# A two-block transformer kernel on one core: negated maxima straight from the masking operation, embedding rows split during the MLP, and the first tables in two loads

## The reference, cut to what matters

```python
# first block, window attention: a softmax with one more "sink" score per head
s = jnp.where(mask, q @ k * d ** -0.5, -jnp.inf)
m = jnp.maximum(jnp.max(s, axis=-1, keepdims=True), sink)
pexp = jnp.exp(s - m)
probs = pexp / (jnp.sum(pexp, axis=-1, keepdims=True) + jnp.exp(sink - m))
# first block, the end of each layer: a gated embedding
gate = jax.nn.sigmoid(_rms_norm(x, ple_norm_g[l]) @ w_ple_gate[l])
e = _rms_norm(p[l] @ w_ple_proj[l], ple_post_norm_g[l])
x = x + gate * e
# second block: three kinds of causal attention, each a softmax over masked scores
p = jax.nn.softmax(jnp.where(kpos <= qpos, s, -jnp.inf), axis=-1)
```

## Time and profile before

| | us |
|---|---|
| median of 3 runs | 3013.02 |
| the profiled execution, its own time | 3004.78 |
| its span, first to last instruction | 3002.9 |
| TensorE busy | 2822.8 (94%) |
| VectorE busy | 1621.1 (54%) |
| ScalarE busy | 1113.5 (37%) |

### The profile page before, as it was taken

One profiled execution on the slowest core, in us unless ns is written; L12 is line 12 of the kernel. 1 busy time (PEld: TensorE's weight loads), 2 busy tenths in 40 slices (PEclk: granted clock), 3 DMA queues, 4 the chain that ended last, 5 costly groups with the idle time before them and its releaser, 6 DMA issues. The chain is left out here.

```text
span 3002.9 us, 37176 instructions
## 1 busy us (share of the span) xinstructions
PE 2822.8 (94%) x14756; PEld 2343.2 (78%) x14756; DVE 1621.1 (54%) x2849; ACT 1113.5 (37%) x1680; POOL 209.8 (7%) x224
## 2 busy tenths in 40 slices
PE   5998899999899889999989999899998998899998
PEld 5877788887788677888777877788887887788887
DVE  5745566655765547655575434553544544464443
ACT  6444322224554433222354444332323344332232
POOL 1320100002120210000120000100000000100001
PEclk9987999999999799999989999999999999999999
DMA  4210154443221014444422110223223210122321
GB/s 154 73 43 29 52 187 168 162 150 117 101 78 57 15 57 168 146 162 168 147 88 84 56 33 25 85 90 105 96 78 105 71 41 27 61 98 73 117 81 67
DMA packets 42835, 278.81 MB, mean 93 GB/s; under 512 B 5928, under 2 KB 6312, under 8 KB 11560
## 3 DMA queue, kind: packets, MB, share of 16 engines
q1 hardware_dynamic: 42664, 276.44, 26.4%
HBM read 274.33 MB, written 2.10 MB: 92 GB/s over the span
## 5 line engine op out<-in xcount | busy, mean ns | idle before, releaser
L307 DVE TENSOR_TENSOR low_panels<-raw_panels,high_panels 128x2048 fp32r<-128x2048 f32 (+3 forms) x218 | 469.3, 2153 | 346.0 <-ACT high_panels L294 345.8
L294 ACT ACTIVATE high_panels<-raw_panels 128x2048 fp32r<-128x2048 f32 (+3 forms) x218 | 392.5, 1802 | 469.0 <-PE bank L1516 150.0
L425 PE MATMUL bank<-mlp_h_high,high_panels 128*128 128x512 f32 x1152 | 451.4, 392 | 0.0
L425 PE MATMUL bank<-mlp_h_high,low_panels 128*128 128x512 f32 x1152 | 450.2, 391 | 0.0
L425 PE MATMUL bank<-mlp_h_low,high_panels 128*128 128x512 f32 x1152 | 448.7, 390 | 0.0
L425 PEld LDWEIGHTS bank<-mlp_h_high,low_panels 128*128 128x128 f32 x1152 | 216.3, 188 | 46.0
L425 PEld LDWEIGHTS bank<-mlp_h_low,high_panels 128*128 128x128 f32 x1152 | 216.4, 188 | 45.9
L425 PEld LDWEIGHTS bank<-mlp_h_high,high_panels 128*128 128x128 f32 x1152 | 216.4, 188 | 44.3
L450 PE MATMUL bank<-high_panels,h_high 128*128 128x256 f32 x704 | 206.5, 293 | 0.5 <-ACT values_and_ones L2033 0.5
L425 PE MATMUL bank<-h_high,high_panels 128*128 128x512 f32 x496 | 204.6, 412 | 0.5 <-DVE h_low L1401 0.3
L1516 PE MATMUL bank<-mlp_hid_high,high_panels 128*128 128x512 f32 x512 | 202.5, 395 | 0.0
(11 more groups left out here) (345 smaller groups left out, 5130.4 us busy)
## 6 DMA issues: line engine op xcount, KB each, us to landing
raw_panels<-in_w SPq DMA_DIRECT2D x236, 1024.0 KB, 4.8
raw_panels<-in_w SPq DMA_DIRECT2D x16, 384.0 KB, 3.2
raw_panels<-in_w SPq DMA_DIRECT2D x4, 960.0 KB, 4.6
raw_panels<-in_w SPq DMA_DIRECT2D x4, 768.0 KB, 4.2
row<-in_row SPq DMA_DIRECT2D x2, 1220.0 KB, 6.2
x<-in_xT SPq DMA_DIRECT2D x2, 1024.0 KB, 6.2
raw_panels<-in_w SPq DMA_DIRECT2D x4, 512.0 KB, 3.6
mix<-in_rope SPq DMA_DIRECT2D x2, 1024.0 KB, 6.2
```

The costliest lines, as they stand in the source:

```text
L294: self.nc.scalar.activation(self.g.high[:, j % SPLIT, 0:raw.shape[1]], raw, ACT.Copy).then_inc(self.high_ready, 1)
L307: self.nc.vector.tensor_tensor(self.g.low[:, j % SPLIT, 0:w], raw, self.g.high[:, j % SPLIT, 0:w].bitcast(F32), ALU.subtract).then_inc(sel ...
L425: ins = nc.tensor.matmul(bank[:, :], w[a][:, k, c0:c0 + P], rhs[b][:, k0 + k, :], start=first and k == 0 and j == 0, stop=last and k == kt ...
```

## The change

It has four parts. (1) In both attentions the mask-and-maximum instruction now multiplies by the negated scale and takes a minimum, so it gives the negated scaled maximum itself; in the window attention the minimum starts from the negated sink. The small VectorE instructions behind it are gone, ScalarE waits for each maximum by itself, and the sinks' exponentials are two ScalarE instructions of one column. (2) The embedding rows are loaded and split in `mlp_one`. (3) In the embedding stage TensorE makes two of the eight embedding groups ahead of the spread of the norm. (4) Start-up loads only the last 8 columns of `k1` and splits only the first panel; the rest of `k1` and the vectors are loaded in the first layer's stage, and the second panel is split inside its norm.

```diff
-                sp.dma_start(k1[:, :], a["k1"]).then_inc(s("tables_loaded"), 16)
+                sp.dma_start(k1[:, L_FREQ:L_WIDTH], a["k1"][:, L_FREQ:L_WIDTH]).then_inc(s("tables_loaded"), 16)
...
-                sp.wait_ge(s("vectors_loaded"), 16 * (2 * DEPTH + 1))
...
-                for i in range(AHEAD):
-                    views[0].low(dve, i)
+                views[0].low(dve, 0)
...
-                for i in range(AHEAD):
-                    views[0].high(act, i)
+                views[0].high(act, 0)
...
@@ layer_one, SP @@
+                if l == 0:
+                    sp.dma_start(k1[:, 0:L_FREQ], a["k1"][:, 0:L_FREQ]).then_inc(s("masks_loaded"), 16)
...
                 pan.loads(sp, AHEAD, 16 + AHEAD)
...
@@ layer_one, window softmax, ACT @@
-                    act.wait_ge(w.neg_ready, p + 1)
                     for m in range(2):
+                        act.wait_ge(w.max_ready, 2 * p + m + 1)
                         o = masked[:, (2 * p + m) % 6, 0:n]
-                        nc.scalar.activation(o, o, ACT.Exp, bias=g.negmax[:, 2 * p + m:2 * p + m + 1], scale=HD ** -0.5).then_inc(w.probs_ready, 1)
-                    act.wait_ge(s("sink_span"), p + 1)
-                    nc.scalar.activation(spans[:, p % 4, :], spans[:, p % 4, :], ACT.Exp).then_inc(s("sink_exp"), 1)
+                        nc.scalar.activation(o, o, ACT.Exp, bias=g.negmax[:, 2 * p + m:2 * p + m + 1], scale=-1.0).then_inc(w.probs_ready, 1)
+                    if p >= 4:
+                        act.wait_ge(w.out_kept, p - 3)
+                    for m in range(2):
+                        c = R_SINK + 2 * j + m
+                        nc.scalar.activation(spans[:, p % 4, m:m + 1], row[:, c:c + 1], ACT.Exp,
+                                             bias=g.negmax[:, 2 * p + m:2 * p + m + 1]).then_inc(s("sink_exp"), 1)
...
-                norm_scalar(nc, act, g, e, hh)
+                norm_scalar(nc, act, g, e, hh, before={3: lambda: pan.high(act, 1)} if l == 0 else None)
...
@@ layer_one, window softmax, DVE @@
-                                                       scale=1.0, scalar=NEG, op0=ALU.add, op1=ALU.max,
-                                                       accum_out=g.rowmax[:, c + m:c + m + 1]).then_inc(w.max_ready, 1)
-                    dve.wait_ge(w.max_ready, c + 2)
-                    st.link(nc.vector.tensor_tensor(g.rowmax[:, c:c + 2], g.rowmax[:, c:c + 2], sinks[:, 2 * j:2 * j + 2], ALU.max))
-                    nc.vector.tensor_scalar(g.negmax[:, c:c + 2], g.rowmax[:, c:c + 2], -HD ** -0.5, None, ALU.mult).then_inc(w.neg_ready, 1)
-                    dve.wait_ge(w.neg_ready, p + 1)
-                    nc.vector.tensor_tensor(spans[:, p % 4, :], g.negmax[:, c:c + 2], row[:, R_SINK + 2 * j:R_SINK + 2 * j + 2], ALU.add).then_inc(s("sink_span"), 1)
+                                                       scale=-HD ** -0.5, scalar=sinks[:, 2 * j + m:2 * j + m + 1], op0=ALU.add, op1=ALU.min,
+                                                       accum_out=g.negmax[:, c + m:c + m + 1]).then_inc(w.max_ready, 1)
...
-                norm_vector(nc, dve, g, e, x, vec[:, V_GIN:V_GIN + DC], hh, hl)
+                norm_vector(nc, dve, g, e, x, vec[:, V_GIN:V_GIN + DC], hh, hl, before={4: lambda: pan.low(dve, 1)} if l == 0 else None)
...
@@ mlp_one @@
+                sp.dma_start(pT[:, :, :], a["p1"][l, :, :, :]).then_inc(s("ple_in"), 16)
...
+                    if i == DC:
+                        act.wait_ge(s("ple_in"), 16)
+                        nc.scalar.activation(ph[:, :, :], pT[:, :, :], ACT.Copy).then_inc(s("p_high"), 1)
...
+                    if i == DC + 2:
+                        dve.wait_ge(s("p_high"), 1)
+                        nc.vector.tensor_tensor(pl[:, :, :], pT[:, :, :], ph[:, :, :].bitcast(F32), ALU.subtract)
...
@@ embedding_gate, PE @@
-                spread_rstd(nc, pe, g, e)
                 w = pan.parts(pe, first)
-                pe.wait_ge(s("p_low"), 1)
                 for c in range(DC):
+                    if c == 2:
+                        spread_rstd(nc, pe, g, e)
                     grp.free(pe, c)
...
@@ layer_two, softmax, ACT and DVE @@
-                    act.wait_ge(w.neg_ready, i + 1)
                     for m in range(2):
+                        act.wait_ge(w.max_ready, 2 * i + m + 1)
...
-                                                       scale=1.0, scalar=NEG, op0=ALU.add, op1=ALU.max,
...
-                    dve.wait_ge(w.max_ready, c + 2)
-                    nc.vector.tensor_scalar(g.negmax[:, c:c + 2], g.rowmax[:, c:c + 2], -u.scale, None, ALU.mult).then_inc(w.neg_ready, 1)
+                                                       scale=-u.scale, scalar=-NEG, op0=ALU.add, op1=ALU.min,
+                                                       accum_out=g.negmax[:, c + m:c + m + 1]).then_inc(w.max_ready, 1)
```

More of the change, by code:

```diff
@@ L490, in _ @@
                     sp.dma_start(lsel[:, i, :], a["lsel"][i, :, :].broadcast_to([P, 2])).then_inc(s("tables_loaded"), 16)
-                sp.dma_start(k1[:, :], a["k1"]).then_inc(s("tables_loaded"), 16)
+                sp.dma_start(k1[:, L_FREQ:L_WIDTH], a["k1"][:, L_FREQ:L_WIDTH]).then_inc(s("tables_loaded"), 16)
                 for n in range(RAW):
                     views[0].stream.load(sp, n)
-                for i in range(DEPTH):
-                    sp.dma_start(gbs[:, i, 0:3], a["gb1"][i, :, :]).then_inc(s("vectors_loaded"), 16)
-                    sp.dma_start(vec2[:, i, :], a["vec2"][i, :, :]).then_inc(s("vectors_loaded"), 16)
-                sp.dma_start(gfin[:, :], a["gfin"]).then_inc(s("vectors_loaded"), 16)
-                sp.wait_ge(s("vectors_loaded"), 16 * (2 * DEPTH + 1))
             st = Steps(s("rope_steps"))
@@ L563, in _, with layer_one @@
                     nc.scalar.activation(bounds[:, i, 3, :], bounds[:, i, 2, :], ACT.Exp)
-                for i in range(AHEAD):
-                    views[0].high(act, i)
+                views[0].high(act, 0)
         for l in range(DEPTH):
-            layer_one(nc, g, a, views[l], l, k1, vecs[:, l, :], row, gbs[:, l, :], cs, bounds[:, l, :, :], small)
-            mlp_one(nc, g, views[l], l, vecs[:, l, :])
-            embedding_gate(nc, g, a, views[l], l, vecs[:, l, :], vec2[:, l, :])
-def layer_one(nc, g, a, pan, l, k1, vec, row, gb, cs, lb, small):
+            layer_one(nc, g, a, views[l], l, k1, vecs[:, l, :], row, gbs, cs, bounds[:, l, :, :], small, vec2, gfin)
+            with ExitStack() as later:
+                pT = later.enter_context(nc.sbuf_tensor(f"ple_pT_{l}", [P, 2, S], F32))
+                ph = later.enter_context(nc.sbuf_tensor(f"ple_p_high_{l}", [P, 2, S], F32R))
+                pl = later.enter_context(nc.sbuf_tensor(f"ple_p_low_{l}", [P, 2, S], F32R))
+                mlp_one(nc, g, a, views[l], l, vecs[:, l, :], pT, ph, pl)
+                embedding_gate(nc, g, views[l], l, vecs[:, l, :], vec2[:, l, :], ph, pl)
+def layer_one(nc, g, a, pan, l, k1, vec, row, gbs, cs, lb, small, vec2, gfin):
     s, used = g.stages.begin()
+    gb = gbs[:, l, :]
     bank, x, nb = g.bank, g.x, g.nb
@@ L711, in _ @@
                 sp.dma_start(row[:, :], a["row1"][l, :, :].broadcast_to([P, R_WIDTH])).then_inc(s("in_vectors"), 16)
+                if l == 0:
+                    sp.dma_start(k1[:, 0:L_FREQ], a["k1"][:, 0:L_FREQ]).then_inc(s("masks_loaded"), 16)
+                    for i in range(DEPTH):
+                        sp.dma_start(gbs[:, i, 0:3], a["gb1"][i, :, :]).then_inc(s("vectors_loaded"), 16)
+                        sp.dma_start(vec2[:, i, :], a["vec2"][i, :, :]).then_inc(s("vectors_loaded"), 16)
+                    sp.dma_start(gfin[:, :], a["gfin"]).then_inc(s("vectors_loaded"), 16)
                 pan.loads(sp, AHEAD, 16 + AHEAD)
+                if l == 0:
+                    sp.wait_ge(s("vectors_loaded"), 16 * (2 * DEPTH + 1))
             @block.gpsimd
@@ L1352, in invert_window @@
                     nc.vector.reciprocal(ss, ss).then_inc(s("w_rstd"), 1)
-                    st.link(nc.vector.tensor_scalar(sinks, row[:, R_SINK:R_SINK + QH], HD ** 0.5, None, ALU.mult))
+                    st.link(nc.vector.tensor_scalar(sinks, row[:, R_SINK:R_SINK + QH], -1.0, None, ALU.mult))
                 def head_squares(v, o, buf):
@@ L1670, in embedding @@
                     nc.scalar.activation(esq[:, c, :], emb[:, c, :], ACT.Square).then_inc(ee.sq_ready, 1)
-                norm_scalar(nc, act, g, e, hh, before={0: p_high, 2: lambda: embedding(0), 3: lambda: embedding(1), 4: lambda: embedding(2),
+                norm_scalar(nc, act, g, e, hh, before={2: lambda: embedding(0), 3: lambda: embedding(1), 4: lambda: embedding(2),
                                                        5: lambda: embedding(3), 6: lambda: embedding(4), 7: lambda: embedding(5)})
```

31 lines of the change are left out of this document (13 added, 18 removed).

## The result

| | before | after |
|---|---|---|
| median | 3012.69 us (4 runs, 3010.84 to 3013.23) | 2966.99 us (4 runs, 2966.08 to 2968.86) |
| ratio | 1 | 0.9859, interval 0.9847 to 0.9872 |
| the profiled execution | 3004.78 | 2967.56 |
| its span | 3002.9 | 2965.6 |
| mean granted clock | 0.958 | 0.963 |

The medians are 45.7 us apart. The ratio and its interval are an estimate over the runs, not the quotient of these two medians (0.9848): 0.9859 stands for 42.5 us, between 38.6 and 46.1. The two profiled executions are only 37.2 apart.

What follows compares the result with a forecast made beforehand. TensorE, busy 94% of the span, was taken as the bound, so only its waits or clock matter; 9.8 + 12.7 + 7.4 + 0.6 = 30.5, taken as 31, from 3013 gives 2982 us, range 2964 to 3001.

Steps and rivals of the forecast that it cites:

- Sum 12.7: Second block's attention: 8 long and 16 short waits for copies of turned probabilities shrink or vanish, 12.7 us of 18.2.
- rival (a): Attentions: shorter waits keep TensorE at the upper clock; 20 us less at the lower gives 10 more, 2972; chance 0.12.
- TensorE's wait for the masking (10.7) stays: Second block's attention: the 10.7 us that TensorE waits for VectorE's masking of the scores was held unchanged.
- Rival (b): Attentions: the next wait, for the masking, takes over; a third of 20.1 stays, total gain 17, or 2996; chance 0.15.
- 9.8 was forecast: Embedding stages, both layers: split rows and 12 products ahead of the spread save 13.0 at full clock, taken as 9.8.
- The 1.6 a layer: Embedding stages: 1.6 us per layer set aside for time still spent at the lower clock.
- 7.4 forecast: Window attention: copy waits lose 5.5 and chunk waits 1.9, sum 7.4 us, between 0 and 13.
- Chunk waits were to lose 1.9: Window attention: the 4 waits for an output projection chunk, 4.6 us, lose 1.9 through the same ScalarE chain.
- 0.2 each: Window attention: upper bound on the masking's new form, 0.2 us per instruction, half exposed, 3 us.
- a masking instruction that got longer: Sign of being wrong: the masking instruction, with its new start value and constant, takes longer.
- 0.1 by the pace: Window attention: one more sink instruction on ScalarE adds 0.1 us per pair by pace, 0.19 by duration.
- 0.6 forecast: Start: splitting one panel instead of two gains 2.2 us, 1.6 is lost in the norm; net 0.6, range -0.7 to 2.2.

Runs made afterwards that it cites:

- e2: Kernel before with only the window attention's negated maxima, on both engines: 3000.32 us, ratio 0.9969.
- e3: Kernel before with only the embedding part, rows split in the MLP and two groups ahead of the spread: 3001.50 us, ratio 0.9977.
- e9: Kernel before with the embedding rows split in the MLP, but the spread still first and no group moved: 3002.47 us, ratio 0.9967.
- e1: Kernel before with only the second block's negated maxima, ScalarE waiting for each maximum by itself: 2990.09 us, ratio 0.9935.
- e4: Changed kernel with the start-up as before, whole table in one load and both first panels split there: 2971.30 us, ratio 0.9875.
- e5: Changed kernel run once more, unedited: 2969.37 us, ratio 0.9873 to the kernel before.
- e7: Changed kernel with the second panel split later, low part behind the first norm, high part before its seventh chunk: 2966.24 us, ratio 0.9856.
- e11: Kernel before with four buffers of masked scores instead of three in the second block, maxima negated as before: 2991.94 us, ratio 0.9940.
- e8: The e7 kernel with four buffers of masked scores instead of three in the second block: 2952.90 us, ratio 0.9811.
- e10: Changed kernel with four buffers of masked scores instead of three in the second block, nothing else: 2949.99 us, ratio 0.9800.
- e6: Kernel before with the second block's negated maxima, but ScalarE waits for both maxima of a pair before the first exponential: 2994.11 us, ratio 0.9957.

## Why the prediction was right, and where it was short

**The second block: right mechanism, term too small.** The step was "the long ones lose 0.8 each, 6.4; the short ones go whole, 6.3. Sum 12.7". The waits did precisely that: 18.2 to 5.4 is 12.8. The attentions still got 23.4 shorter. To see why, this stage needs more than one execution. Without the edit it stands in four profiled executions (before, e2, e3, e9), twice in each; with it, and nothing else in that block, in five (after, e1, e4, e5, e7). Beside the mean length stands the mean time that the record of the granted clock has at the lower level within the stage:

| | lengths | mean | lower clock in it, mean |
|---|---|---|---|
| without | 333.8, 335.5, 339.4, 340.1, 340.3, 340.5, 342.2, 342.3 | 339.3 | 27.4 |
| with | 324.7, 326.5, 327.8, 328.0, 328.0, 328.2, 328.3, 328.8, 329.5, 331.0 | 328.1 | 18.6 |

The length goes with the clock inside each group too. The shortest and the longest one without the edit stand in one execution, e2, 8.3 us apart, with 13.0 and 35.0 us of the lower clock. As stretches of e2 (length, PE busy, granted clock):

```profile
1569.11:1902.95 333.84, 309.34 (x1924) 0.98 0.18 60
2276.08:2618.23 342.15, 318.76 (x1924) 0.95 0.17 56
```

TensorE is busy 9.4 us longer in the second and idle no longer (24.5 and 23.4 us), so here it is the clock that makes the length. A least-squares line through the eight gives 0.39 us of length for each us at the lower clock, 0.44 through the ten. At equal clock, 18 us of it, the lines stand at 335.6 and 327.8: 7.8 per layer, 15.6 for both. The means are 11.2 per layer apart; the other 3.4 go with 8.8 us less at the lower clock. So 12.7 was too small twice: by 2.9, of which 2.1 are the masking waits that the prediction held fixed, and by some 7 that the clock gave on top. This division is an estimate by the two lines; no run holds the clock fixed. That is rival (a), "if 20 us less are spent at the lower level, 10 us more". It came true in this place, with a price a little lower (17.6 us less in the two layers, for 7), but it was given a chance of 0.12 and stood beside the forecast with nothing of it in the term. With the edit the two layers together have 29.7 to 46.3 us of the lower clock in the five executions, without it 47.9 to 59.5 in the four. Over the whole kernel the record has 253 us at the lower clock before and 218 after.

The clock does not come with every wait that goes. The fourth buffer alone (e11) took 16.6 us of TensorE's waits in this block (6.8 for the copies, 9.8 for the masking), more than the maxima did, and left 58.8 us at the lower clock in the two layers, as much as before; its gain, 16.8 us, is the waits and no more. Why the maxima bring clock and the buffer doesn't no run here tells.

The argument against rival (a) was that 17.1 us at the lower clock "followed a mere few waits". That stretch says little either way: it is 17.1 us again in the changed kernel, but over the thirteen executions it lasts 10.2, 13.7 or 17.1, with the old code of the window attention (10.2 in e11, 13.7 in e1) as with the new (10.2 in e2, 13.7 in e7).

**"TensorE's wait for the masking (10.7) stays: nothing is taken away between the scores and the masked scores."** Failed. The masking waited for a buffer, the buffer for TensorE's turning, and that for the exponential which now starts early. Rival (b) of the prediction had this in its "against" ("the masking starts from TensorE's own turning, which moves with it"), but the sum did not use it. The wait was in the view of before, at the step of the earlier trace rows, and was not followed back:

```profile
1776.09 0.69 DVE L2157 CUSTOM_DVE_ANT_0 masked_scores<-bank,k 128x512 f32<-128x512 f32 x1 [0.79 <-PE bank L1958]
...
1776.85 0.49 PE L1944 MATMUL bank<-q_and_k 64*128 64x128 f32 x4 [0.57 <-DVE stats L2157]
```

The edit itself took only 2.1 to 2.8 us of the masking waits. e8, e10 and e11 show what the buffer behind them was worth: 13 to 17 us, more than the 12.7 at which the largest term of the sum was forecast.

**The embedding stage: right in size, half of the reason idle.** 9.8 was forecast; the stages of the two layers together last 145.3 before and 136.5 after, 8.8 less. In other executions the pair takes 144.6 to 146.7 without the edits (e1, e2, e6, e11) and 133.3 to 135.0 with both (e3, e4, e5, e7, e8, e10), 11.8 less by the means, near the 13.0 that was worked out for the full clock. From the root to the first gate product it was to be 12.2 us (739.6 less 727.4); it is 13.6 in the changed kernel, with 3.4 us of the lower clock in it, and 12.0 in e10. The 1.6 a layer that the term set aside for the clock is what the changed kernel shows. But that half of the working that moved 12 products into the gap is worth nothing in the end: in e9, with the spread first, the gate products start at 12.6 and the pair takes 133.0. No new wait came, as forecast. Timed alone it gave 6.6 (e3) and 8.1 (e9), whose intervals reach from 4 to 14 us; they are not at odds with 11.8, and do not prove it.

**The window attention: right in sum, two of its terms off.** 7.4 forecast, 7.8 by e2. Chunk waits were to lose 1.9 and lost 0.2 (0.9 in e2); the copies' lost 5.4 of the 5.5 (6.1 in e2). The masking's new form did cost: with its start value read from a column it takes 479 ns where it took 418 for 128x256 and 345 where it took 284 for 128x128. In the second block, where the start value is a constant, it stayed at 688 against 687. From each view the rows (mean ns behind the busy us), before and after:

```profile
L1376 DVE CUSTOM_DVE_ANT_0 arena<-bank,k 128x256 f32<-128x256 f32 x48 | 18.3, 418 | 0.0
```

```profile
L1389 DVE CUSTOM_DVE_ANT_0 arena<-bank,k,small 128x256 f32<-128x256 f32 x48 | 21.2, 479 | 0.4 <-PE bank L919 0.4
```

64 of these at 0.06 are 3.9 us of VectorE, against the bound of "0.2 each"; how much of it TensorE waits for was not measured. The prediction had named a masking instruction that got longer as a sign of being wrong; it came, and was too small to turn the result. The sinks cost more than the "0.1 by the pace" as well. Their rows before and after:

```profile
L1108 ACT ACTIVATE small<-small 128x2 f32<-128x2 f32 x32 | 6.0, 188 | 0.0
```

```profile
L1118 ACT ACTIVATE small<-row,stats 128x1 f32<-128x1 f32 x64 | 14.9, 279 | 0.0
```

A pair's sinks take 0.47 of ScalarE's busy time instead of 0.19.

**The start: 0.6 forecast, 1.9 to 4.3 by the timed runs, which their spread does not tell from nothing.** In the trace the stage ends 2.2 earlier as forecast, and the fourth chunk waits 0.58 where up to 1.6 was expected to be lost; e7 took that wait away and gained nothing that can be told.

**The time it was set against.** The prediction subtracted from 3013, the median of before's first runs. The 51 later runs of before have medians of 3008.1 to 3010.5, so some 2 to 4 of the 45.7 us are the luck of those first runs; the ratio stands for 42.5, and on another set of runs the change gave 40.3. Before's own runs lie between 3002 and 3017, and they go with the mean granted clock: a line through the 51 gives about 2.3 us for each 0.001 (three of them: 3003.89 at 0.959, 3008.01 at 0.957, 3016.75 at 0.955). The profiled execution of before, 3004.78, is shorter than 45 of the 51, and its layer 1 attention took 324.2 where the same code took 325.3 to 330.2 in e1, e3, e6, e9 and e11, and 316.5 to 326.3 in seven executions with the new form. So 45.7 less is not 31 and one missing term. By the means over the executions that share a stage's code, the change takes 22.4 in the second block's attentions (forecast 12.7), 11.8 in the embedding stages (9.8), 8.8 in the first block's attentions (7.4) and 2.2 at the start (0.6). The MLPs of the second block give about 3 back, which leaves 42. In the one behind the second block's first attention the clock takes it: 372.4 to 373.3 us there in before, e1, e2, e3, e6, e9 and e11, with 10 to 11 us of the lower clock, and 375.0 to 375.4 in after, e4, e5, e7, e8 and e10, with 16 to 17. None of the three parts alone does this (e1, e2, e3); why all together do stays open.

The rows bear on a rule of the Trainium skill, "TensorE: Matmul & The Clock Gate", Terms: the penalty is about the time throttled times (1 - K/N), which for half the clock is one half. The stages here show 0.39 and 0.44, so for the 35 us of the lower clock that went over the whole kernel, the rule has 17.5 and the two slopes 14 to 15, an estimate that carries them over to the other stages. Why they lie below one half no run here tells.

**The sum of the parts.** The three alone give 18.0 + 7.8 + 6.6 = 32.4, and the changed kernel with the old start gave 36.8 on the same chip and against the same runs of before. The parts add up within their intervals; nothing hints at one that pays only with the others.

## What to carry to other kernels

When a wait is shortened, follow the engine behind it to what it waits for in turn: here VectorE's 0.79 us for a buffer, written in the view, was worth nearly as much as the whole edit in that block (17 and 18 us, each alone), and one more buffer took it. Where short waits go, the time won can be the waits alone (16.6 of waits and 16.8 of time in e11) or the waits and nearly half as much again by the clock (15.6 and 7 with the maxima), so give the term a range that holds both, instead of leaving the clock to a rival. And when the clock differs from one execution to the next, compare a stage over all the executions that have it unchanged; one profile of before may be its best.

## What the runs showed that was not expected

- One stage, the same code for both layers in one execution: 333.84 and 342.15 us (e2), with 13.0 and 35.0 us at the lower clock. A stage's difference between two profiles below some 8 us says nothing by itself.
- The mask-and-maximum instruction is 61 ns longer when its start value is a column, at 128 and at 256 columns alike, and no longer with the negated scale and the minimum.
- Two ScalarE instructions of one column for a pair's sinks, 64 of 279 ns (14.9 us busy), replaced 32 of 188 ns with two columns (6.0), and no row of the view has an engine waiting for them.
- The wait that a view names and the buffer that it hangs on can be on different engines: with three buffers of masked scores 50 of the 160 maskings waited for TensorE's turning before the change and 56 after it, none with four, in a kernel whose masked-score wait on TensorE was only the sixth row.
